# Expert rows fetched as U and V side by side, one gather per pair, and weights made four experts at a time

## The reference

```python
def peer(h, w_query, sub_keys, expert_u, expert_v):
    q = (hf @ w_query).reshape(T, PEER_HEADS, 2, PEER_HALF)
    scores = jnp.einsum("thpd,hpnd->thpn", q, sub_keys)
    top_v, top_i = lax.top_k(scores, PEER_TOPK)          # 16 of each half
    ...                                                  # 16 x 16 sums, the 16 best of them
    best_v, best_pos = lax.top_k(cand_v, PEER_TOPK)
    expert_idx = jnp.take_along_axis(cand_i, best_pos, axis=-1)
    gates = jax.nn.softmax(best_v, axis=-1)
    def body(xc):
        u = jnp.take(expert_u, xc["idx"], axis=0)
        vv = jnp.take(expert_v, xc["idx"], axis=0)
        a = jax.nn.gelu(jnp.einsum("td,thkd->thk", xc["h"], u))
        return jnp.einsum("thk,thkd->td", xc["g"] * a, vv)

# in second_block, for each of the two layers l
x = x + g2 * peer(h, w_query[l], sub_keys[l], expert_u[l], expert_v[l])
```

## Time and profile before

| | us |
|---|---|
| median of 3 runs | 2652.36 (2651.65 to 2652.45) |
| span of the profiled execution | 2650.5 |
| up to the first gather of layer 1 | 924.55 |
| first expert stage, first gather to the start of its last V's addition | 924.55 to 1668.63 |
| second expert stage, its last V's addition | 2633.86 |

### The profile page before, as it was taken

How to read it: one execution, slowest core, us unless ns; L and a number is a source line. 1 busy time by engine, 2 the same in 40 slices (tenths; PEclk the granted TensorE clock), 3 DMA queues, 4 the chain that set the end, 5 groups by cost and what they waited for, 6 DMA issues and landing times. The chain is left out here.

```text
span 2650.5 us, 25842 instructions
## 1 busy us (share of the span) xinstructions
PE 2159.8 (81%) x8779; PEld 1348.7 (51%) x8779; DVE 1635.8 (62%) x3179; ACT 771.9 (29%) x1599; POOL 1067.8 (40%) x1121
## 2 busy tenths in 40 slices
PE   6789999899899978777777677799898877767665
PEld 5578857688697654433222222587553333222221
DVE  6578845588756567756645644565677655555644
ACT  4445444444445222111121111354132112102110
POOL 0001010010002056666666667020366666666664
PEclk9899989999999989898889999899898989898999
DMA  7078832489554399999999999835599999999997
GB/s 257 34 267 312 314 101 104 175 303 335 206 186 154 105 376 352 363 376 357 392 362 363 367 378 375 313 137 175 218 354 359 368 362 368 368 364 380 360 359 292
DMA packets 244430, 774.87 MB, mean 292 GB/s; under 512 B 20362, under 2 KB 24874, under 8 KB 244323
## 3 DMA queue, kind: packets, MB, share of 16 engines
q0 software_dynamic: 160512, 587.27, 58.6%
q1 hardware_dynamic: 83810, 186.25, 19.7%
HBM read 772.35 MB, written 1.10 MB: 292 GB/s over the span
## 5 line engine op out<-in xcount | busy, mean ns | idle before, releaser
L2790 PE MATMUL experts_fourth<-experts_v_slot,experts_diagonal 128*128 128x512 f32 x896 | 454.3, 642 | 188.0 <-issue 96.5
L2344 POOL DMA_INDIRECT experts_v_slot<-in_expert_v_dram,experts_at x496 | 476.4, 960 | 316.3 <-issue 135.2
L2790 PE MATMUL experts_first<-experts_v_slot,experts_diagonal 128*128 128x512 f32 x1024 | 497.1, 628 | 86.5 <-issue 44.9
L2790 PEld LDWEIGHTS experts_fourth<-experts_v_slot,experts_diagonal 128*128 128x128 f32 x896 | 165.2, 200 | 477.0 <-issue 466.7
L2790 PEld LDWEIGHTS experts_first<-experts_v_slot,experts_diagonal 128*128 128x128 f32 x1024 | 194.1, 199 | 356.0 <-issue 349.3
L2555 DVE CUSTOM_DVE_ANT_0 ring<-ring,experts_second 128x1024 f32<-128x1024 f32 x192 | 234.2, 1220 | 191.0 <-DMA ring<-in_expert_u_dram,experts_at 161.4
L2339 POOL DMA_INDIRECT ring<-in_expert_u_dram,experts_at x312 | 295.6, 947 | 103.1 <-issue 89.6
L561 POOL DMA_DIRECT2D mlp_ada_half<-in_w_ada_dram x48 | 36.3, 757 | 538.8 <-DVE csum L684 317.8
L2672 ACT ACTIVATE experts_dots<-experts_dots 128x16 f32<-128x16 f32 x32 | 6.9, 217 | 722.4 <-DVE experts_dots L2555 370.7
L187 DVE TENSOR_TENSOR mix_lo<-ring,mix_hi 128x1024 fp32r<-128x1024 f32 x96 | 132.1, 1383 | 125.5 <-ACT mix_hi L2067 125.4
L2555 DVE CUSTOM_DVE_ANT_0 ring<-ring,experts_third 128x1024 f32<-128x1024 f32 x120 | 144.3, 1219 | 87.4 <-DMA ring<-in_expert_u_dram,experts_at 70.9
(11 more groups left out here) (463 smaller groups left out, 4228.0 us busy)
## 6 DMA issues: line engine op xcount, KB each, us to landing
mlp_ada_half<-in_w_ada_dram POOLq DMA_DIRECT2D x48, 1024.0 KB, 8.1
ring<-in_w_in_dram SPq DMA_DIRECT2D x20, 2048.0 KB
ring<-in_mlp_w_in_dram SPq DMA_DIRECT2D x16, 2048.0 KB
ring<-in_mlp_w_out_dram SPq DMA_DIRECT2D x16, 2048.0 KB
ring<-in_w_query_dram SPq DMA_DIRECT2D x8, 2048.0 KB
ring<-in_gla_w_in_dram SPq DMA_DIRECT2D x6, 2048.0 KB
ring<-in_w_out_dram SPq DMA_DIRECT2D x4, 2048.0 KB
experts_v_slot<-in_expert_v_dram,experts_at POOLq DMA_INDIRECT x496
```

The source lines that it names most:

```text
L2344: pool.indirect_dma_start(v_row(n, j), None, rows_v, bass.IndirectOffsetOnAxis(ap=at[:, n, j:j + 1], axis=0)).then_inc(v_landed(n, j), 16)
L2790: mm = pe.matmul(y[n // PH][:, b, :], diagonal[n % 2][:, j, :], v_row(n, j)[:, b * HALF:(b + 1) * HALF], start=n % PH == 0 and j == 0, sto ...
```

## The change

The host lays U and V of an expert side by side: a new table `experts_uv` of shape layer x expert x 2 x 1024, in which an expert is one row of 8 KB. One gather brings both into a **pair slot**. There are 13 slots, and pair i (of 256, i = 16 n + j) takes slot i mod 13; up to pair 116 (`BORROWED` = 117) two of them are `xn` and `K.mod`, later two are ring space. The space comes from the 8 V slots, one of the two sets of diagonals (now `extra`), `u_first`, `shared` and the ring. A pair's slot is given out again when TensorE has used its V (`v_used`).

Weights are made in groups of four pairs: GELU of four dots, the weights of a group two dots into the next one (at once at the end of units 0, 1, 2 and 15), four diagonals, four V rows. The 16 diagonals are one set. Late projections stand between groups, in ScalarE's and TensorE's order. VectorE adds only the last two V rows itself. The loads that waited for the dots of half the units or for the last landing now wait for `v_used`.

```diff
-    VS = 8
+    PAIRS = 13
+    GROUP = 4
-    BY_DVE = range(VS)
+    BY_DVE = range(ALL - 2, ALL)
-    BORROWED = PH
+    BORROWED = 9 * PAIRS
-        diagonal = [st.sb(f"diagonal{n}", [P, TOPK, P]) for n in range(2)]
+        diagonal = st.sb("diagonal", [P, TOPK, P])
+        extra = st.sb("extra", [P, 2, D])
...
+        early = [flat(u_first[:]), flat(v_slot[:, 0:2, :]), flat(v_slot[:, 2:4, :]), flat(v_slot[:, 4:6, :]),
+                 flat(extra[:]), flat(shared[:]), flat(v_slot[:, 6:8, :]), flat(xn[:]), flat(K.mod[:]),
+                 *(ring_pair(panels[n // 2], n % 2) for n in range(4))]
+        late = early[0:7] + [ring_pair(panels[2], n) for n in range(2)] + early[9:]
...
-                    sp.wait_ge(dots_done, UNITS * TOPK)
-                    sp.wait_ge(v_landed(LAST, TOPK - 1), v_arrived(LAST, TOPK - 1))
+                    sp.wait_ge(v_used, ALL // PAIRS * PAIRS)
                     start_panels(sp, K, following)
...
+                def gather(i):
+                    n, j = divmod(i, TOPK)
                     pool.indirect_dma_start(
+                        pair(i), None, rows,
+                        bass.IndirectOffsetOnAxis(ap=at[:, n, j:j + 1], axis=0)).then_inc(pair_in[i % PAIRS], 16)
                 pool.wait_ge(first_eight, 1)
+                for i in range(5):
+                    gather(i)
                 pool.wait_ge(res_done, 2 * T)
+                gather(5)
+                pool.wait_ge(x_done, 2 * T)
+                gather(6)
                 pool.wait_ge(at_ready, 1)
                 pool.wait_ge(h2_there, T)
                 pool.wait_ge(xn_done, 2 * T)
+                for i in (7, 8):
+                    gather(i)
                 pool.wait_ge(q_done, PH + 4)
+                for i in (9, 10):
+                    gather(i)
+                pool.wait_ge(q_done, EARLY)
+                for i in (11, 12):
+                    gather(i)
+                for i in range(PAIRS, ALL):
+                    n, j = divmod(i, TOPK)
+                    if j == 0:
+                        pool.wait_ge(at_ready, n + 1)
+                    if i == BORROWED + 7:
+                        pool.wait_ge(q_done, EARLY + PH + 4)
+                    pool.wait_ge(v_used, i - PAIRS + 1)
+                    gather(i)
...
-                        dve.wait_ge(u_in[j], 16 * n + 16)
+                        dve.wait_ge(pair_in[i % PAIRS], pair_arrived(i))
...
+                        if j % GROUP == 1 and i // GROUP > weighed[0]:
+                            weigh(i // GROUP - 1)
+                    if flush:
+                        weigh(i // GROUP)
...
+                    for k in range(TOPK // GROUP):
+                        g = n * TOPK // GROUP + k
+                        act.wait_ge(dots_done, GROUP * g + GROUP)
+                        some = dots[:, n, k * GROUP:(k + 1) * GROUP]
+                        act.activation(some, some, ACT.Gelu_apprx_tanh).then_inc(gelu_done, 1)
+                        act.wait_ge(weight_done, g + 1)
+                        if g * GROUP >= TOPK:
+                            act.wait_ge(v_used, GROUP * (g + 1) - TOPK)
...
+                        if k < len(late):
+                            move_queries(late[k])
+                        if 1 <= k <= len(late):
+                            move_scores(late[k - 1])
...
+                    for k in range(TOPK // GROUP):
+                        if 1 <= k <= len(late):
+                            score(late[k - 1])
+                        if k < len(late):
+                            project_step(late[k])
+                        weighted(n, k)
...
+    ins["experts_uv"] = declare("experts_uv", _np.stack([inputs["expert_u_2"], inputs["expert_v_2"]], axis=2))
```

More of the change, by code:

```diff
@@ L2287, in experts, with ring_pair, flat, pair @@
                      "act_own", "dve_own"))
[L2289 to L2310, removed]
+        def ring_pair(panel, n):
+            return K.ring[:, panel % SLOTS, n * 2 * D:(n + 1) * 2 * D]
+        def flat(a):
+            return a.rearrange("p a d -> p (a d)")
+        early = [flat(u_first[:]), flat(v_slot[:, 0:2, :]), flat(v_slot[:, 2:4, :]), flat(v_slot[:, 4:6, :]),
+                 flat(extra[:]), flat(shared[:]), flat(v_slot[:, 6:8, :]), flat(xn[:]), flat(K.mod[:]),
+                 *(ring_pair(panels[n // 2], n % 2) for n in range(4))]
+        late = early[0:7] + [ring_pair(panels[2], n) for n in range(2)] + early[9:]
+        def pair(i):
+            return (early if i < BORROWED else late)[i % PAIRS]
+        def u_row(i):
+            return pair(i)[:, 0:D]
+        def v_row(i):
+            return pair(i)[:, D:2 * D]
+        def pair_arrived(i):
+            return 16 * (i // PAIRS + 1)
         with nc.Block() as block:
@@ L2547, in choose_beside, with unit @@
                                           ALU.add).then_inc(at_ready, 2)
-                def unit(n, beside=None):
+                def unit(n, beside=None, flush=False):
                     if n % PH == 0:
@@ L2781, in score, with weighted @@
                               start=True, stop=True).then_inc(scored, 1)
-                def rows(n, some):
-                    for j in some:
-                        if n == LAST and j in BY_DVE:
+                def weighted(n, k):
+                    for j in range(k * GROUP, (k + 1) * GROUP):
+                        i = n * TOPK + j
+                        if i in BY_DVE:
                             continue
-                        pe.wait_ge(diagonal_ready, TOPK * n + (j + 1 - VS if n == LAST else j + 1))
-                        pe.wait_ge(v_landed(n, j), v_arrived(n, j))
+                        pe.wait_ge(diagonal_ready, i + 1)
                         for b in range(2):
-                            mm = pe.matmul(y[n // PH][:, b, :], diagonal[n % 2][:, j, :],
-                                           v_row(n, j)[:, b * HALF:(b + 1) * HALF],
+                            mm = pe.matmul(y[n // PH][:, b, :], diagonal[:, j, :],
+                                           v_row(i)[:, b * HALF:(b + 1) * HALF],
                                            start=n % PH == 0 and j == 0, stop=False, skip_group_check=True)
```

145 lines of the change are left out of this document (43 added, 102 removed).

## The result

| | kernel before | changed kernel |
|---|---|---|
| median | 2652.09 us (2651.65 to 2652.45, 4 runs) | 2495.45 us (2493.94 to 2502.36, 4 runs) |
| profiled span | 2650.5 | 2492.3 |

The larger finding came later. **In other sessions the kernel before runs at 2510 us, and the change gains only 0.6%.** The chip is not what differs: two chips were each in a session of the one kind and later in one of the other. The result on record is of the kind in which the kernel before takes 2652, and so is the trace on which the prediction rests.

A forecast was written before the change was run, and what follows sets the result against it. The prediction took the expert stages as bound by a stream of gathers losing 76 us a layer to stops. Savings of 52.2 and 59.6 us in the two layers gave 2538.7 profiled, 2541 us median; range 2501 to 2625.

The forecast's parts named there:

- Bytes and rate: Expert-stage gathers: equal bytes, 8 KB rows at 421 GB/s, 2.50 us a pair against 2.56, 15 us a layer.
- The loss before: First expert stage of the kernel before: 688 us less 478 gathers of 1.28 us, 76 us lost to stops.
- GpSimd: Gather issue in the expert stage: 256 instead of 512 a layer, 0.94 + 0.30 us each, at most 2.2 us.
- The start: Start of each expert stage: pair 13 waits for the first used slot until 979.4; four pairs, 10 us a layer, lost.
- no idle at all: Range's low end: the main case without its 20 us of idle in either layer, 2501 us.
- The idle: Expert stages: 20 us idle a layer, 8 at the list block before unit 3, 12 for remaining stops; bounds 0 and 76.
- TensorE: V rows in the expert stage: pauses may lower its clock, but a group needs 8.7 of 10 us, still covered.
- The end: Last landing to sum: 5.7 us, 4.4 more than before, plus 3 for the next layer's panels in the first layer.
- the largest term: Expert stages: pair slots deepen the queue, covering stops of 2 to 6 us; at most 76 us a layer to win.
- Rival B: Expert-stage gathers: 8 KB rows cut into two 4 KB transfers, 2.56 us a pair, 15 us a layer back, 2570 us; chance 0.17.
- C: Expert stages: stops persist in part, half of the 76 us a layer stays, 2577 to 2650 us; chance 0.22.
- Rival D: Pair slots in the expert stages: 13 too few, transfers wait for slots, 2650 us and up; chance 0.08.

The follow-up runs named there:

- undisturbed run: Kernel before, unedited, run and profiled again in a session where it takes about 2510 us, not the 2652 to 2659 of disturbed sessions: 2512.0 us.
- pairs_9: Changed kernel with 9 pair slots instead of 13: 2760.0 us, beside a kernel before at 2509.
- rows_4k: Changed kernel with each pair slot filled by two gathers of 4 KB rows, 13 slots kept: 2532.5 us beside kernel before at 2509, 2712.5 beside 2656.

## Why the prediction was partly right

The sum was made against the profiled span, 2538.7 for 2492.3: 46.4 us too much. By its own steps:

- *Bytes and rate*: right. 2.49 us a pair, the extrapolated value (2.50 taken), 2.4 us a layer over. The rival of rows cut in two was wrong. The rule of the Trainium skill quoted there (DMA: Bandwidth & Descriptors, SWDGE vs HWDGE vs iDMA: a packet of at most 4096 B is preferred) was not borne out here: 8 KB packets ran at 421 GB/s, 4 KB ones at 410 (and 409 in the undisturbed run above).
- *The loss before*: read a little high. The 76 us count gathers alone; by bytes, 370 of 410 GB/s, it is 67 us, since other loads share the stretch.
- *GpSimd*: right. 0.94 us for a gather of twice the bytes.
- *The start*: wrong, and the step that failed. By the prediction it took 54.9 us from the first gather to pair 13 in the first layer (979.4 - 924.55) and 56.3 in the second; it was 45.2 and 45.8. The places of the pairs and of the first used row were read from a stretch with stops in it, as if they were set by work. The gather into `xn` was issued at 952.99, 28.4 us after the first; here it comes after 21.2, and in the undisturbed kernel before after 21.1. TensorE's first row starts 53.1 us after the first gather in the trace that was read (977.62) and 45.6 in the undisturbed one: 7.5 us of stops. In the changed kernel it starts after 43.0, 2.6 earlier with groups of four. The error is 9.7 and 10.5 us, 20 of the 46, and the term had no range of its own. So the low end, "no idle at all", was no low end.
- *The idle*: 20 us a layer forecast, and near by luck. Between restart and last landing 15 and 10 us are left over 243 pairs of 2.49 (in the first layer 1586.3 - 965.9 - 605.1), but most of the 15 is not idle: 4.4 MB of other loads moved there, 10 us at 421 GB/s, and 0.5 MB, 1 us, in the second layer. With all loads the DMA engines moved 418 and 416 GB/s over these stretches, so some 4 to 8 us a layer were lost. The 20 was made of a list block of 26.3 us and of stops; without stops the block takes 15.2. Its 4.5 us from issue to landing had no row: a pair took 14.5 us with the queue deep, and in pairs_9, with 9 slots, medians of 5.7 to 8.7 us by place in 1500 to 1540 us.
- *TensorE*: right that its clock doesn't matter. The granted clock was 0.92 in 1200 to 1400 us where the undisturbed kernel before had 0.98, and the transfers set the pace in both. Not every group started slow: the first row took 1.98 us at 1512.33 and 3.68 at 1522.73. The rule of the Trainium skill quoted there (TensorE: Matmul & The Clock Gate, HAM oscillation) is on bursts shorter than the wait for their data; these are longer, 7.1 us to about 3.
- *The end*: 5.7 us forecast from the last landing to the sum, 6.3 and 7.6 measured. The 3 us for the next layer's panels did not come as a term of their own, between the layers; but 2.4 MB of panels moved beside the last pairs, in 1570 to 1586 us, 5.7 us at 421 GB/s, and are within the 15 above.
- *Not in the sum*: 6 us ahead of the first gather (924.55 to 918.59), in code that the change doesn't touch. Every kernel with pair slots had them, at 917.4 to 921.9; the old one was at 924.6 and 925.9. The difference grows in small steps through the first stack, to 7.2 us at ScalarE's move at 727.42 us in the undisturbed kernel before (720.20 in the changed one). The cause is open.

These make 6.0 + 9.7 + 10.5 for the two starts and what is ahead of them, 7.1 and 12.7 behind them in the layers (5 and 10 of it for the 20 us, 2.4 each rate), 3.0 for the panels, less 0.6 and 1.9 at the ends: 46.5, the 46.4 but for rounding.

The mechanism of the largest term was wrong as well. The forecast took the stops as given, some 76 us a layer, and let a deeper queue cover all but 20. The queue got deep, but there was nothing for it to cover: the stops did not happen. With the same slots and 512 gathers they came back, and rows_4k took 180 us more in the disturbed session than undisturbed, where the kernel before took some 145 more. And "it can hardly build a queue" was wrong: the old kernel's queue stands at 17.3 us when nothing stops it. The 76 us were a property of the session as much as of the kernel.

Undisturbed, the account is small. Of the spans 2510.5 and 2491.9, 7.1 us lie ahead of the first gather, and 5.6 and 5.3 in the two expert stages (679.7 to 674.1 and 675.4 to 670.1 from first gather to sum). One gather of 8 KB rows for two of 4 KB gives 40 us in all (spans of rows_4k 2532.2, changed 2491.9), some 34 of them by the rate (486 pairs of 2.49 us for 2.56). The slots and the groups of four cost 29 us back (40.3 + 7.1 - 18.6). The start takes about 12 of these, where the transfers wait for the first used slot: in the first 120 us from the second layer's first gather GpSimd's queue moves 42.3 MB in rows_4k and 44.7 in the kernel before, 6 us at 409 GB/s, and in the first layer as much. The ends take 13: from the last landing to the sum it is 6.7 and 9.2 us in rows_4k, 1.3 in the kernel before.

Rival B did not come, and C neither: no part of the stops was left. Rival D (a ring too short) did not come, but its arithmetic was wrong as well. Its turn of "16.5 + 4.5 us" was added up along one pair, where a loop through the next group sets the time; it would have given 9 slots 2.5 us a pair where they take 3.0. At 13 slots the error didn't show.

## What to carry to other kernels

Before sizing a gain from stops that the profile can't name, run the kernel in another session: if they are gone there, the gain belongs to the session. Where slots are given back through a group, don't add up one item's time; find the loop (which later item must land before this group is released) and count how many groups it spans. One gather of a long row for two of short ones halves what GpSimd issues, and in disturbed sessions that was worth some 160 us: adding as many tiny gathers cost 200 (2697.7 for 2498.1, in two sessions), of which undisturbed they cost 38 (2534.0 for 2496.2).

## What the runs showed of the hardware

A gather of 128 rows of 8 KB takes GpSimd 0.94 us to issue, as one of 4 KB. Eight-KB rows move at 421 GB/s, 4 KB rows at 409 to 410, and 8 KB rows with a 64 B row behind each at 412 (a gather of 128 such tiny rows stands in the records as 16 packets of 512 B). A transfer of 128 rows of 64 B by SyncE stands there as 128 packets of 64 B. Whole sessions slow one program by 6% and leave another, which does the same work with half the gathers, within 0.2%. The granted clock of the whole execution goes with it for the first, 0.94 to 0.95 for 0.97, and stays at 0.94 for the second.

Instruction fetch was a suspect for the stops. The Trainium skill (Runtime: NRT & Kernel Launch, Instruction fetch mechanics) says that instructions arrive in blocks of 16 KB. The transfer queues on the page of the profile agree in size, 0.95 MB in 58 packets being 16.4 KB each; here they are for the kernel before in the first session and in the undisturbed one (packets, MB, share):

```profile
q8 instruction: 58, 0.95, 0.1%
```

```profile
q8 instruction: 58, 0.95, 0.2%
```

The same 58 packets with stops and without: nothing here lays the stops on it, though equal counts don't rule it out.
